# Routed experts: up weights split on chip into two float32r parts, three passes in place of one float32 product

## The chip, the cores and the metric

The kernel runs on one core of one Trainium2 chip. The metric is the device time of one execution in microseconds, taken as the median of several runs. All the times of instructions below come from one profiled execution.

## The reference, cut to what matters

The program is one inference step of a two-layer decoder trunk for 576 tokens (512 of a prompt and 64 of a sample group), width 1024. Layer 0 has a dense feed-forward part, layer 1 one of eight experts, of which each token uses two. Only this last part is touched:

```
def swiglu(x, w1, w3, w2):
    return (jax.nn.silu(x @ w1) * (x @ w3)) @ w2

    def moe(x, e_layer):
        ...
        logits = (xf @ moe_router[e_layer]).astype(f32)
        top_v, top_i = lax.top_k(logits, TOP_K)
        gw = jax.nn.softmax(top_v, axis=-1)
        comb = jnp.sum(jax.nn.one_hot(top_i, N_EXPERTS, dtype=f32) * gw[..., None], axis=1)
        y = jnp.zeros_like(xf)
        for e in range(N_EXPERTS):
            y = y + comb[:, e:e + 1].astype(x.dtype) * swiglu(xf, moe_w1[e_layer, e], moe_w3[e_layer, e], moe_w2[e_layer, e])
```

An expert has w1 and w3 of 1024 x 1408 (the "up" weights) and w2 of 1408 x 1024 ("down").

## The kernel before, in words

The tokens are sorted by expert into 16 blocks of 128 slots (`NBK`), written to `d_xs` by indirect DMAs, and each block is then run with the weights of its expert, which are read from HBM anew for each block. An expert's number is only known at run time, so SP loads it into a register ahead of each block.

A block's weights come in 18 units of up to 1 MiB (128 partitions x 2048 float32). Twelve are up units: groups g = 0, 1, 2 of 512, 512 and 384 hidden columns (`FG`), each with two halves q of the 1024 inputs and with w = 0, 1 for w1 and w3. The up units of group 2 are 1536 columns wide. Six are down units of two 128-row chunks f of w2 each, the last of one chunk. All of them go through one ring of 11 slots (`ring`), in the order in which PE uses them; SP issues unit n as soon as PE has finished unit n - 11 (`moe_used`).

In a block PE's order is written out in `moe_pe`: up 0, up 1, the transposes hT 0, up 2, hT 1, down 0, the transposes xT of the next block's tokens, hT 2, down 1, down 2. The tokens are the stationary operand (`XBT`) and the weights move. `moe_up_pe` (L2112) makes 4 matmuls per unit, 8 per PSUM bank. ACT takes Silu of the bank of w1 (`silu`, L2167), DVE multiplies it with the bank of w3 into `he_buf` (L2207), PE transposes that (hT, L2124), ACT copies it to `ht_buf` (`turned`, L2172), PE multiplies with the down weights (L2139). ACT copies the block's result (L2185) and sends it to `d_ys`. DVE prepares the next block's tokens from xT (L2197). Every engine runs its own instructions strictly in the order written; semaphores alone tie them together.

The dense layer 0 has long been computed with split operands: L470 multiplies float32r parts of the weights and of the tokens, 288 columns a time, in three passes (rounded x rounded, rounded x rest, rest x rounded). There ACT makes the rounded part (L455) and POOL or DVE the rest (L458, L533).

Of the kernel before, what the change touches and what calls it, by code (L numbers as in the profile page):

```python
# [14 lines left out]
P = 128  # L15
D = 1024
# [23 lines left out]
BLOCK_UNITS = UP_UNITS + DN_UNITS  # L40
RING = 11
# [144 lines left out]
def build(nc, A):  # L186

    with ExitStack() as ctx:
# [8 lines left out]
        SECOND = ("cmp_", "rope_", "at_", "sa_", "cw", "pages_", "qpages_", "qwin", "wo_", "w_out_", "ffn_norm", "moe_")  # L197
        shared, used = [], {True: 0, False: 0}

        def S(name):  # L200
            if name not in sems:
                part = name.startswith(FIRST)
                if part or name.startswith(SECOND):
# [50 lines left out]
        ring = put_at("ring", RING * 2048, mr)  # L254
        xn_tok = put_at("xn_tok", 5 * D, mx)
        xbt_buf = put_at("xbt_buf", 2 * D, mx)
        yb_buf = put_at("yb_buf", 2 * D, mx + 2 * D)
# [7 lines left out]
        wbc_buf = put_at("wbc_buf", 2 * D, mc + 13312)  # L265
        slot_buf = put_at("slot_buf", 16, mc + 15360, I32)
        ebt_buf = put_at("ebt_buf", NBK, mc + 15376, I32, 1)
        assert RING * 2048 <= 2560 + ARENA and 15392 <= NCH * T
# [1599 lines left out]
        XBT = xbt_buf[:, :].rearrange("p (m k t) -> p m k t", m=2, t=P)  # L1868
# [184 lines left out]
        def unit_of(b, u):  # L2053
            return (b * BLOCK_UNITS + u) % RING, (b * BLOCK_UNITS + u) // RING

        def up_unit(g, q, w):
            return 4 * g + 2 * q + w

        def moe_sp():
# [4 lines left out]
            for b in range(NBK):  # L2064
# [9 lines left out]
                for u in range(BLOCK_UNITS):  # L2074
                    slot, turn = unit_of(b, u)
                    if turn:
                        sp.wait_ge(S("moe_used"), b * BLOCK_UNITS + u - RING + 1)
                    if u < UP_UNITS:
                        g, q, w = u // 4, u // 2 % 2, u % 2
                        src = A["moe_up"][e * 8 + u] if g < 2 else A["moe_up2"][e * 4 + (u - 8)]  # L2080
                    else:
                        src = A["moe_dn"][e * DN_UNITS + (u - UP_UNITS)]
                    n = 2048 if u < 8 or u >= UP_UNITS else 4 * FG[2]
                    if u == BLOCK_UNITS - 1:
                        src, n = src[:, 0:D], D
                    sp.dma_start(ring[:, 2048 * slot:2048 * slot + n], src).then_inc(S(f"moe_unit_{slot}"), 16)
# [11 lines left out]
        def moe_up_pe(b, g):  # L2098
# [7 lines left out]
            for q in range(2):  # L2106
                for w in range(2):
                    u = up_unit(g, q, w)
                    slot, turn = unit_of(b, u)
# [17 lines left out]
        def moe_down_pe(b, g):  # L2127
# [4 lines left out]
            for f in range(4 * g, min(4 * g + 4, FC)):  # L2132
                u = UP_UNITS + f // 2
                slot, turn = unit_of(b, u)
                if f % 2 == 0:
                    pe.wait_ge(S(f"moe_unit_{slot}"), 16 * (turn + 1))
# [607 lines left out]
```

## Time and profile before

| | |
|---|---|
| median of 3 runs | 3269.13 us (3267.05 to 3274.06) |
| profiled execution | 3268.38 us, span 3266.6 us |
| PE busy in the span | 2788.6 us (85%) |
| DVE, ACT, POOL busy | 1121.7, 546.0, 356.0 us |
| float32 matmuls of the up weights (L2112) | 611.9 us busy, 1536 records |
| float32 matmuls of the down weights (L2139) | 307.4 us busy, 704 records |

Busy times are those of the engine over the whole span. A float32 matmul shows as two records with a weight load each, so 768 matmuls of the up weights are 1536 records. A float32r matmul shows as one record. In the chain of waits the first number of a row is its start in us from the span's start, the second how long it lasted.

### The profile page before, as it was taken

The page shows a single profiled execution, that of the slowest core. Times are in us where ns is not written, and L with a number is a line of the kernel's source. Part 1 is how long each engine was busy: PE and PEld are TensorE (multiplying, and loading weights), DVE is VectorE, ACT ScalarE, POOL GpSimd, SP SyncE. Part 2 cuts the span into 40 slices and gives each one's busy share as a digit, 9 for nine tenths or more (in the row PEclk, how much of TensorE's full clock was granted, in tenths as well). Part 3 has the DMA queues.
Part 4 walks back from the last instruction along what each step waited for, and adds up shares of the span by engine and source line. Part 5 has one row for each costly group of instructions (what it writes and reads, how often), then busy time and mean ns, then how long its engine had stood idle before and what let it go on. Part 6 is the DMA issues. An engine that isn't in the chain of part 4 may idle for free.

```text
span 3266.6 us, 36648 instructions
## 1 busy us (share of the span) xinstructions
PE 2788.6 (85%) x14880; PEld 2010.0 (62%) x14894; DVE 1121.7 (34%) x1676; ACT 546.0 (17%) x820; POOL 356.0 (11%) x160
## 2 busy tenths in 40 slices
PE   7977686897869999899648778885999999999994
PEld 6965583544769999799538654464454444544442
DVE  5314856367332032251376545843000000000002
ACT  3331100122222122222320011232000000000001
POOL 2320000000233333133000000011000000000001
PEclk9985786797889999899568878877999999999997
DMA  3210201210122343121012023013999988888883
GB/s 143 80 40 31 90 1 69 81 30 14 40 84 89 107 154 97 35 84 60 13 46 76 1 82 98 13 40 139 378 318 310 318 306 314 318 305 317 311 306 112
DMA packets 114970, 445.01 MB, mean 136 GB/s; under 512 B 12722, under 2 KB 47410, under 8 KB 86258
## 3 DMA queue, kind: packets, MB, share of 16 engines
q1 hardware_dynamic: 109874, 424.84, 38.0%
q0 software_dynamic: 2624, 9.44, 0.9%
q10 hardware_dynamic: 2304, 8.39, 0.6%
q8 instruction: 118, 1.93, 0.2%
q14 instruction: 50, 0.41, 0.0%
HBM read 410.28 MB, written 40.59 MB: 138 GB/s over the span
## 4 chain that ended last, share of the span: by engine, by line
PE 78%; DVE 15%; ACT 2%; issue 2%; DMA 1%; POOL 1%; DVEq 0%; SPq 0%; ACTq 0%; POOLq 0%; PEldq 0%
PE ps_buf L470 27%; PE ps_buf L2112 19%; PE ps_buf L2139 9%; PE ps_buf L1042 3%; PE ps_buf L1325 2%; PE ps_buf L1486 2%; PE ps_buf L1434 1%; PE ps_buf L1445 1%; PE ps_buf L1033 1%; DVE cols_buf L1140 1%; PE ps_buf L741 1%; PE ps_buf L1451 1%; PE ps_buf L1635 1%; DVE h_buf L529 1%; PE ps_buf L2124 1%
## 5 line engine op out<-in xcount | busy, mean ns | idle before, releaser
L470 PE MATMUL ps_buf<-xh_buf,whl_buf 128*128 128x288 f32 x3648 | 655.2, 301 | 71.1 <-POOLq L163 35.6
L2112 PE MATMUL ps_buf<-ring,xbt_buf 128*128 128x512 f32 (+1 forms) x1536 | 611.9, 558 | 3.4 <-DMA ring<-d_moe_up 3.4
L470 PEld LDWEIGHTS ps_buf<-xh_buf,whl_buf 128*128 128x128 f32 x3648 | 545.9, 191 | 79.8 <-issue 61.5
L2112 PEld LDWEIGHTS ps_buf<-ring,xbt_buf 128*128 128x128 f32 x1536 | 291.3, 191 | 313.0 <-issue 249.4
L470 PE MATMUL ps_buf<-xl_buf,whl_buf 128*128 128x288 f32 x1824 | 397.1, 299 | 0.0
L458 POOL TENSOR_TENSOR whl_buf<-arena,whl_buf 128x1024 fp32r<-128x1024 f32 (+1 forms) x114 | 289.0, 2535 | 582.6 <-ACTq L163 582.0
L2139 PE MATMUL ps_buf<-ring,ht_buf 128*128 128x512 f32 x704 | 307.4, 592 | 0.0
L470 PEld LDWEIGHTS ps_buf<-xl_buf,whl_buf 128*128 128x128 f32 x1824 | 297.8, 192 | 0.0
L2207 DVE TENSOR_TENSOR he_buf<-se_buf,ps_buf 128x512 f32<-128x512 f32 (+1 forms) x48 | 30.9, 644 | 769.1 <-ACT se_buf L2167 769.1
L2139 PEld LDWEIGHTS ps_buf<-ring,ht_buf 128*128 128x128 f32 x704 | 131.3, 190 | 153.1 <-issue 153.1
L455 ACT CAST whl_buf<-arena 128x1024 fp32r<-128x1024 f32 (+1 forms) x114 | 125.0, 1096 | 538.2 <-PE ps_buf L470 531.0
L458 POOL TENSOR_TENSOR whl_buf<-cols_buf,whl_buf 128x1024 fp32r<-128x1024 f32 x16 | 39.9, 2494 | 1264.9 <-ACTq L163 1264.5
L2167 ACT ACTIVATE se_buf<-ps_buf 128x512 f32<-128x512 f32 (+1 forms) x48 | 27.0, 562 | 595.5 <-PE ps_buf L2112 595.5
L470 PE MATMUL ps_buf<-hh_buf,whl_buf 128*128 128x288 f32 x704 | 122.9, 296 | 0.0
L2049 POOL DMA_INDIRECT yg_buf<-d_ys,slot_buf x10 | 9.4, 938 | 974.2 <-DMA d_ys<-yb_buf 958.4
L470 PEld LDWEIGHTS ps_buf<-hh_buf,whl_buf 128*128 128x128 f32 x704 | 103.4, 188 | 0.0
L2299 DVE TENSOR_TENSOR cols_buf<-arena,ps_buf 128x576 f32<-128x576 f32 x22 | 16.6, 755 | 211.4 <-PE ps_buf L470 211.4
L470 PE MATMUL ps_buf<-cols_buf,tab 128*128 128x288 f32 x144 | 50.6, 513 | 36.4 <-ACTq L163 15.7
L1486 PE MATMUL ps_buf<-arena,h_buf 128*128 128x512 f32 (+3 forms) x256 | 77.4, 447 | 2.5 <-ACTq L163 2.5
L1161 DVE TENSOR_TENSOR cols_buf<-cols_buf,ps_buf 128x512 f32<-128x512 f32 (+1 forms) x94 | 63.0, 670 | 43.5 <-PE ps_buf L1042 36.7
L470 PE MATMUL ps_buf<-hl_buf,whl_buf 128*128 128x288 f32 x352 | 75.7, 296 | 0.0
L1325 PE MATMUL ps_buf<-arena 128*128 128x296 f32 x256 | 69.9, 439 | 6.3 <-issue 6.3
(475 smaller groups left out, 3120.3 us busy)
## 6 DMA issues: line engine op xcount, KB each, us to landing
ring<-d_moe_up SPq DMA_DIRECT2D x128, 1024.0 KB, 7.2
ring<-d_moe_dn SPq DMA_DIRECT2D x80, 1024.0 KB, 7.0
ring<-d_moe_up SPq DMA_DIRECT2D x64, 768.0 KB, 6.5
arena<-d_w_in SPq DMA_DIRECT2D x54, 512.0 KB, 3.6
arena<-d_w SPq DMA_DIRECT2D x44, 512.0 KB, 3.7
arena<-d_w SPq DMA_DIRECT2D x16, 704.0 KB, 4.1
arena<-d_pages_c SPq DMA_DIRECT2D x64, 128.0 KB, 2.1
cols_buf<-d_w_out SPq DMA_DIRECT2D x16, 512.0 KB, 3.6
```

Source lines behind the costliest of these rows:

```text
L455: a(nc.scalar.copy(part(slot, 0, nk, size), src), *sig)
L458: g(nc.gpsimd.tensor_tensor(part(slot, 1, nk, size), src, part(slot, 0, nk, size).bitcast(F32), ALU.subtract), *sig)
L470: last = nc.tensor.matmul(ps_buf[0:rows, b + a_, 0:HALF], w, m[:, a_ * HALF:(a_ + 1) * HALF], start=start, stop=stop)
L529: v(ve.scalar_tensor_tensor(dst, x[:, k, :], w(k), rs, ALU.mult, ALU.mult), S(tag + ("_done" if final else "_scaled")))
L741: pe.matmul(o, onehot(h, n), R[0:4, RU, t0:t0 + n], start=True, stop=False)
L1033: last = pe.matmul(ps_buf[0:n, 4 * s_, q * n:q * n + n], M1[s_][0:n, q, 0:n], Dm[s_][0:n, q * n:q * n + n], start=True, stop=True)
L1042: last = pe.matmul(ps_buf[0:n, 4 * s_ + b, c], l_[s_][0:n, c], r_[s_][0:n, c], start=True, stop=True)
L1161: v(ve.tensor_tensor(D[s_][0:n, 0:4 * n], D[s_][0:n, 0:4 * n], ps_buf[0:n, 4 * s_ + b, 0:4 * n], ALU.add), *sig)
L1325: last = pe.matmul(bank(4 * j + 2 * g + half, 9 * 32 + 8), cw1[:, j, 8 * half + p_, :], ckb[:, :, j, g, 8 * p_:8 * p_ + 8], start=p_ == 0, ...
L1486: last = pe.matmul(ps_buf[:, out_banks(u) + g, P * c:SEQ], vaug[:, w, c, P * g:P * g + P], PTs[:, u % 2, g, CHUNK_AT[c]:CHUNK_AT[c] + n], ...
L2112: last = pe.matmul(ps_buf[:, o + w, 0:n], XBT[:, b % 2, 4 * q + k, :], ring[:, 2048 * slot + n * k:2048 * slot + n * k + n], start=q == 0 ...
L2139: last = pe.matmul(ps_buf[:, 6 + h, 0:512], HT[:, b % 2, f, :], ring[:, at:at + 512], start=f == 0, stop=f == FC - 1)
```

## The change

The up weights are no longer multiplied as float32. ACT copies each landed up unit to a float32r buffer (`high`, the rounded part), DVE subtracts this from the raw unit into a second one (`low`, the rest). PE multiplies in three passes with the rounded tokens `XBH` and their rest `XBL`. Down stays as it was. There are 4 raw up slots, 5 raw down slots and 3 pairs of split buffers in place of the ring of 11. A raw up slot is free when DVE has made its rest (`moe_lo`), a split pair when PE has used it (`moe_used`), a down slot when PE has used it (`moe_dn_used`). Tokens are split by DVE with two more operations per block. Some semaphores take over those of the dense layer, which are cleared by then.

```diff
@@ buffers
-ring = put_at("ring", RING * 2048, mr)                 # RING = 11
+up_buf = put_at("up_buf", RAW_UP * 2048, mr)           # RAW_UP, RAW_DN, SPLITS = 4, 5, 3
+dn_buf = put_at("dn_buf", RAW_DN * 2048, mr + RAW_UP * 2048)
+split_bufs = [...]                                     # three of 4096 columns, F32R
@@ moe_sp: the units of block b, in this order
-                for u in range(BLOCK_UNITS):
-                    slot, turn = unit_of(b, u)
-                    if turn:
-                        sp.wait_ge(S("moe_used"), b * BLOCK_UNITS + u - RING + 1)
...
+                for u in range(UP_UNITS):
+                    n = UP_UNITS * b + u
+                    if n >= RAW_UP:
+                        sp.wait_ge(S("moe_lo"), n - RAW_UP + 1)
+                    sp.dma_start(raw_up(n), A["moe_up"][e * 8 + u] if u < 8 else A["moe_up2"][e * 4 + (u - 8)])\
+                        .then_inc(S(f"moe_up_{n % RAW_UP}"), 16)
+                for u in range(DN_UNITS):
+                    m = DN_UNITS * b + u
+                    cols_n = D if u == DN_UNITS - 1 else 2 * D
+                    if m >= RAW_DN:
+                        sp.wait_ge(S("moe_dn_used"), m - RAW_DN + 1)
...
@@ moe_up_pe
-                    pe.wait_ge(S(f"moe_unit_{slot}"), 16 * (turn + 1))
+                    pe.wait_ge(S("moe_lo"), u + 1)
                     for k in range(4):
-                        last = pe.matmul(ps_buf[:, o + w, 0:n], XBT[:, b % 2, 4 * q + k, :],
...
+                        for x_, half in ((XBH, 0), (XBH, 1), (XBL, 0)):
+                            last = pe.matmul(ps_buf[:, o + w, 0:n], x_[:, b % 2, 4 * q + k, :], up_part(u, half)[:, c],
...
@@ moe_act
+            def high(n):
+                if n < UP_UNITS * NBK:
+                    ac.wait_ge(S(f"moe_up_{n % RAW_UP}"), 16 * (n // RAW_UP + 1))
+                    if n >= SPLITS:
+                        ac.wait_ge(S("moe_used"), n - SPLITS + 1)
+                    ac.copy(up_part(n, 0), raw_up(n)).then_inc(S("moe_hi"), 1)
+
+            for n in range(SPLITS):
+                high(n)
             for b in range(NBK):
+                n = UP_UNITS * b + SPLITS
+                for i in range(3):
+                    high(n + i)
                 silu(b, 0)
+                for i in range(3, 7):
+                    high(n + i)
                 silu(b, 1)
+                high(n + 7)
                 turned(b, 0)
+                for i in range(8, 11):
+                    high(n + i)
                 silu(b, 2)
+                high(n + 11)
                 turned(b, 1)
                 turned(b, 2)
@@ moe_dve
+                v(ve.tensor_tensor(XBT, src, nffn.unsqueeze(2).to_broadcast([P, KD, P]), ALU.mult))
+                v(ve.tensor_copy(XBH[:, b % 2], XBT))
+                v(ve.tensor_tensor(XBL[:, b % 2], XBT, XBH[:, b % 2].bitcast(F32), ALU.subtract), S("moe_xbt"))
+            def low(n):
+                if n < UP_UNITS * NBK:
+                    ve.wait_ge(S("moe_hi"), n + 1)
+                    ve.tensor_tensor(up_part(n, 1), raw_up(n), up_part(n, 0).bitcast(F32), ALU.subtract)\
+                        .then_inc(S("moe_lo"), 1)
...
+                for i in range(3, 7):
+                    low(n + i)
+                gated(b, 1)
+                for i in range(7, 11):
+                    low(n + i)
+                gated(b, 2)
+                low(n + 11)
                 if b + 1 < NBK:
                     xbt(b + 1)
```

Three places of the instruction order are shown. The first is ACT's, in one block from the second Silu to the copy of the result, before (`part_92` is `moe_used`, `part_61` is `moe_h`, `part_62` is `moe_hT`):

```order
L2167 ACTIVATE se_buf<-ps_buf 128x512 [waits part_61,part_92] x2
L2172 COPY ht_buf<-ps_buf 128x512 [waits part_62]
L2167 ACTIVATE se_buf<-ps_buf 128x384 [waits part_61,part_92]
L2172 COPY ht_buf<-ps_buf 128x512 [waits part_62]
L2172 COPY ht_buf<-ps_buf 128x384 [waits part_62]
L2185 COPY yb_buf<-ps_buf 128x1024 [waits part_92]
```

And the same place now (`part_76` to `part_79` are the landings `moe_up_0` to `moe_up_3`, `part_80` is `moe_used`, `part_47` is `moe_hT`, `part_46` is `moe_h`):

```order
L2187 ACTIVATE se_buf<-ps_buf 128x512 [waits part_46,part_80]
L2200 CAST split_buf_72<-up_buf 128x1536 [waits part_80,part_78]
L2192 COPY ht_buf<-ps_buf 128x512 [waits part_47]
L2200 CAST split_buf_73<-up_buf 128x1536 [waits part_80,part_79]
L2200 CAST split_buf_71<-up_buf 128x2048 [waits part_80,part_76]
L2200 CAST split_buf_72<-up_buf 128x2048 [waits part_80,part_77]
L2187 ACTIVATE se_buf<-ps_buf 128x384 [waits part_46,part_80]
L2200 CAST split_buf_73<-up_buf 128x2048 [waits part_80,part_78]
L2192 COPY ht_buf<-ps_buf 128x512 [waits part_47]
L2192 COPY ht_buf<-ps_buf 128x384 [waits part_47]
```

Between the copy of group 0 and the third Silu (128x384) there are now three casts; the two that are 2048 wide are up units 0 and 1 of the next block.

The second place is DVE's, around the third product of a block (`he_buf` 128x384), now (`ex_raw_free` is `moe_hi`, `ex_h` is `moe_silu`); before, only the three products and one `xbt_buf` operation stood in a block:

```order
L2250 TENSOR_TENSOR he_buf<-se_buf,ps_buf 128x512 [waits part_47,ex_h]
L2242 TENSOR_TENSOR split_buf_72<-up_buf,split_buf_72 128x1536 [waits ex_raw_free]
L2242 TENSOR_TENSOR split_buf_73<-up_buf,split_buf_73 128x1536 [waits ex_raw_free]
L2242 TENSOR_TENSOR split_buf_71<-up_buf,split_buf_71 128x2048 [waits ex_raw_free]
L2242 TENSOR_TENSOR split_buf_72<-up_buf,split_buf_72 128x2048 [waits ex_raw_free]
L2250 TENSOR_TENSOR he_buf<-se_buf,ps_buf 128x384 [waits part_47,ex_h]
L2242 TENSOR_TENSOR split_buf_73<-up_buf,split_buf_73 128x2048 [waits ex_raw_free]
L2235 TENSOR_TENSOR xbt_buf<-ps_buf,small 128x1024 [waits ex_raw_in_1]
L2236 CAST xbh_buf<-xbt_buf 128x1024 [waits dve_chain]
L2237 TENSOR_TENSOR xbl_buf<-xbt_buf,xbh_buf 128x1024 [waits dve_chain]
```

Here too the rests of units 0 and 1 of the next block stand ahead of this block's third product.

The third place is SP's, from a block's last down unit to the next block's first up unit, now (`part_82` is `moe_dn_used`, `ex_out_free` is `moe_lo`):

```order
L2105 ISA [waits part_82]
L2105 DMA dn_buf<-d_moe_dn 128x1024
L2084 TENSOR_LOAD ebt_buf
L2084 ISA x2
L2091 DMA xb_buf<-d_xs 128x1024 [waits ex_raw_in_1]
L2097 ISA [waits ex_out_free]
L2097 DMA up_buf<-d_moe_up 128x2048
```

The order of the transfers is that of before; what the last down unit waits for is new: with five down slots it is the block's own first down unit, where it was the use of the eleventh unit back.

## Rows read from the trace of the kernel before

**Rows 1.** The chain of waits, from the experts' start: start us, length us, engine, line

```profile
2271.45 7.50 DMA ring<-d_moe_up
2279.08 29.68 PE ps_buf L2112 x64
2309.20 10.32 PE ps_buf L2112 x32
...
2340.05 27.47 PE ps_buf L2112 x64
2367.95 10.32 PE ps_buf L2112 x32
...
2398.80 27.47 PE ps_buf L2112 x64
```

**Rows 2.** Groups by line and form: xcount | busy us, mean ns of one

```profile
L2112 PE MATMUL ps_buf<-ring,xbt_buf 128*128 128x512 f32 x1024 | 444.1, 594 | 3.4 <-DMA ring<-d_moe_up 3.4
L2207 DVE TENSOR_TENSOR he_buf<-se_buf,ps_buf 128x384 f32<-128x384 f32 x16 | 8.9, 554 | 159.4 <-ACT se_buf L2167 159.4
```

**Rows 3.** Timeline of PE, layer 1's output projection: eight times x4 and x2 between

```profile
2180.88 0.70 PE L470 MATMUL ps_buf<-xh_buf,whl_buf 128*128 128x288 f32 x4
2181.41 0.43 PE L470 MATMUL ps_buf<-xl_buf,whl_buf 128*128 128x288 f32 x2
...
2187.28 0.43 PE L470 MATMUL ps_buf<-xh_buf,whl_buf 128*128 128x288 f32 x2
```

**Rows 4.** Groups by line and form: wide operations of ACT and DVE in SBUF

```profile
L455 ACT CAST whl_buf<-arena 128x1024 fp32r<-128x1024 f32 x98 | 102.9, 1050 | 436.5 <-PE ps_buf L470 429.3 <-DMA arena<-d_w 6.8
L455 ACT CAST whl_buf<-arena 128x1408 fp32r<-128x1408 f32 x16 | 22.0, 1377 | 101.7 <-PE ps_buf L470 101.7
...
L533 DVE TENSOR_TENSOR xl_buf<-h_buf,xh_buf 128x576 fp32r<-128x576 f32 x24 | 18.2, 758 | 3.5
L1850 DVE CAST xh_buf<-split_buf 128x576 fp32r<-128x576 f32 x16 | 11.4, 714 | 0.6
L1231 DVE TENSOR_TENSOR arena<-arena,small 128x1024 f32<-128x1024 f32 x4 | 4.9, 1224 | 0.1
L1254 DVE TENSOR_TENSOR h_buf<-h_buf,small 128x1280 f32<-128x1280 f32 x4 | 6.0, 1492 | 0.1
L2301 DVE TENSOR_TENSOR hl_buf<-cols_buf,hh_buf 128x576 fp32r<-128x576 f32 x22 | 55.0, 2499 | 0.8
```

**Rows 5.** Timeline of a block's down part, steady state

```profile
2613.55 7.03 PE L2139 MATMUL ps_buf<-ring,ht_buf 128*128 128x512 f32 x16
2620.42 1.04 PE L2095 MATMUL ps_buf<-tab,xb_buf 128*128 128x128 f32 x8
2621.30 0.49 PE L2124 MATMUL ps_buf<-tab,he_buf 128*128 128x128 f32 x3
2621.62 12.18 PE L2139 MATMUL ps_buf<-ring,ht_buf 128*128 128x512 f32 x28
```

**Rows 6.** Timeline of the experts' first transfers and first work

```profile
2270.45 0.33 SPq L2068 DMA_DIRECT2D xb_buf<-d_xs  x1
2270.82 0.43 SPq L2072 DMA_DIRECT2D xb_buf<-d_xs  x1
2271.45 13.80 SPq L2086 DMA_DIRECT2D ring<-d_moe_up  x12
2273.73 1.97 PE L2095 MATMUL ps_buf<-tab,xb_buf 128*128 128x128 f32 x8 [23.21 <-DMA xb_buf<-d_xs]
2279.08 6.51 PE L2112 MATMUL ps_buf<-ring,xbt_buf 128*128 128x512 f32 x10 [3.38 <-DMA ring<-d_moe_up]
```

**Rows 7.** Stretches: busy us of PE, PEld, DVE, ACT, POOL; granted clock, DMA share, GB/s

```profile
2271.00:2280.00 9.00, 2.89 (x9) 2.07 (x10) 1.23 (x1) 0.00 (x0) 0.00 (x0) 0.50 0.92 362
2280.00:2290.00 10.00, 10.00 (x21) 4.39 (x20) 0.00 (x0) 0.00 (x0) 0.00 (x0) 0.85 1.01 426
2290.00:2300.00 10.00, 10.00 (x24) 4.37 (x23) 0.69 (x1) 0.60 (x1) 0.00 (x0) 1.00 1.01 416
...
2457.00:2516.00 59.00, 59.00 (x161) 28.68 (x160) 3.16 (x4) 4.19 (x7) 0.00 (x0) 1.00 0.91 312
```

More of the change, by code:

```diff
@@ L39 @@
 DN_UNITS = 6
-BLOCK_UNITS = UP_UNITS + DN_UNITS
-RING = 11
+RAW_UP, RAW_DN, SPLITS = 4, 5, 3
 NEG = -1e30
@@ L202, in S @@
                 part = name.startswith(FIRST)
+                if name.startswith("moe_") and FFN_ONLY:
+                    sems[name] = S(FFN_ONLY.pop())
+                    return sems[name]
                 if part or name.startswith(SECOND):
@@ L2051, in moe_gather_pool, with up_cols, raw_up, up_part @@
                         .then_inc(S(f"moe_yg_{i % 2}"), 16)
-        def unit_of(b, u):
-            return (b * BLOCK_UNITS + u) % RING, (b * BLOCK_UNITS + u) // RING
+        def up_cols(n):
+            return 2048 if n % UP_UNITS < 8 else 4 * FG[2]
+        def raw_up(n):
+            return up_buf[:, 2048 * (n % RAW_UP):2048 * (n % RAW_UP) + up_cols(n)]
+        def up_part(n, which):
+            return split_bufs[n % SPLITS][:, 2048 * which:2048 * which + up_cols(n)]
         def up_unit(g, q, w):
@@ L2107, in moe_up_pe @@
                 for w in range(2):
-                    u = up_unit(g, q, w)
-                    slot, turn = unit_of(b, u)
-                    pe.wait_ge(S(f"moe_unit_{slot}"), 16 * (turn + 1))
+                    u = UP_UNITS * b + up_unit(g, q, w)
+                    pe.wait_ge(S("moe_lo"), u + 1)
                     for k in range(4):
-                        last = pe.matmul(ps_buf[:, o + w, 0:n], XBT[:, b % 2, 4 * q + k, :],
-                                         ring[:, 2048 * slot + n * k:2048 * slot + n * k + n],
-                                         start=q == 0 and k == 0, stop=q == 1 and k == 3)
+                        c = slice(n * k, n * k + n)
+                        for x_, half in ((XBH, 0), (XBH, 1), (XBL, 0)):
+                            last = pe.matmul(ps_buf[:, o + w, 0:n], x_[:, b % 2, 4 * q + k, :], up_part(u, half)[:, c],
+                                             start=q == 0 and k == 0 and x_ is XBH and half == 0,
+                                             stop=q == 1 and k == 3 and x_ is XBL)
                     last.then_inc(S("moe_used"), 1)
@@ L2132, in moe_down_pe @@
             for f in range(4 * g, min(4 * g + 4, FC)):
-                u = UP_UNITS + f // 2
-                slot, turn = unit_of(b, u)
+                m = DN_UNITS * b + f // 2
                 if f % 2 == 0:
-                    pe.wait_ge(S(f"moe_unit_{slot}"), 16 * (turn + 1))
+                    pe.wait_ge(S(f"moe_dn_{m % RAW_DN}"), 16 * (m // RAW_DN + 1))
                 for h in range(2):
-                    at = 2048 * slot + D * (f % 2) + 512 * h
-                    last = pe.matmul(ps_buf[:, 6 + h, 0:512], HT[:, b % 2, f, :], ring[:, at:at + 512],
+                    at = 2048 * (m % RAW_DN) + D * (f % 2) + 512 * h
+                    last = pe.matmul(ps_buf[:, 6 + h, 0:512], HT[:, b % 2, f, :], dn_buf[:, at:at + 512],
                                      start=f == 0, stop=f == FC - 1)
                 if f % 2 or f == FC - 1:
-                    last.then_inc(S("moe_used"), 1)
+                    last.then_inc(S("moe_dn_used"), 1)
         def moe_pe():
```

62 lines of the change are left out of this document (35 added, 27 removed).

## The prediction

> **What bounds the kernel now.** I read the chain of waits first, then the groups by line, then a timeline of one block, then the stretches. The chain [rows 1] shows that the experts' part is one unbroken row of PE work: up 0 and 1 (27.47 us), up 2 (10.32), down, and again, with a period of 2398.80 - 2340.05 = 58.75 us for each of 16 blocks. The only wait for a transfer is the first, 3.4 us in all [rows 2]. The stretches say the same: PE is busy throughout at the full clock of 2.4 GHz, the DMA engines move 312 GB/s (the last stretch) [rows 7], and ACT and DVE are nearly idle. Right at the start the same engines moved 416 to 426 GB/s, so the steady 312 is what PE asks for and not what they can do. 312 GB/s over 58.75 us are 18.3 MB a block; at 420 GB/s they would take 43.7 us. So PE's passes bound this part, and anything that makes PE wait is added to the time.
>
> **What the change removes: PE passes.** A block has 64 + 32 records for up, together 27.47 + 10.32 = 37.79 us [rows 1]; that is 0.429 us a record of 512 columns, two records a matmul. Now each of the 32 + 16 matmuls is three float32r passes: 96 of 512 columns and 48 of 384. No row shows a float32r pass of 512. The nearest is 288: between 2180.88 and 2187.28 stand 48 of them, 6.40 / 48 = 133.3 ns each [rows 3], where 288 columns at 2.4 GHz are 120. The excess of 13.3 ns may be fixed (226.7 and 173.3 ns), may grow with the columns (237 and 178 ns), or may be the weight load's and vanish behind a longer pass (213.3 and 160 ns). I take it as fixed, the middle: 96 x 0.2267 + 48 x 0.1733 = 30.1 us, 7.7 us less a block, 123 us in 16 blocks. The ends are 31.3 us (6.5 less, 104 in all) and 28.2 us (9.6 less, 154 in all).
>
> The Trainium skill, "TensorE: Matmul & The Clock Gate", section "Back-to-back issue gap", gives N/2.4 + 2.5 ns for a matmul at full clock. That would be 122.5 ns at 288, and the trace has 133.3, so it does not agree for these passes; with it the up part would be 28.5 us and the total 25 us below mine.
>
> **What it adds on ACT and DVE, in the steady flow.** ACT casts took 1050 ns for 1024 columns and 1377 for 1408, so 0.852 ns a column: 1.92 us for 2048 and 1.49 for 1536. DVE took 1224 ns for 1024 and 1492 for 1280: 1.047 ns a column, 2.30 us and 1.76 us. That its float32r results cost no more is seen at 576 columns, 758 ns. All of this is [rows 4]. A split pair goes round cast, rest, PE and four hand-overs of some 0.1 us: 1.92 + 2.30 + 12 x 0.2267 + 0.3 = 7.2 us, with three pairs 2.4 us a unit, against PE's 2.72. So within a block the splits stay just ahead of PE. Per block ACT gets 8 x 1.92 + 4 x 1.49 = 21 us and DVE 25 us and some 2 us for the tokens, in a period of over 50. Cost there: none. Its bounds: zero, or, if DVE ran as in its slowest row (2499 ns for 576 [rows 4], in a part of the kernel where POOL works beside it; POOL is idle here [rows 7]), far more; that is a rival below.
>
> **What it adds by its order: one stall a block.** This is the term that decides. Three facts from the order of instructions and the code meet:
>
> 1. SP's transfers are in order, and the last down unit of block b (the sixth, with five slots) waits until PE has used the first down unit of the same block. All of block b+1's transfers stand behind it. Call this moment t0.
> 2. ACT's third Silu of block b stands behind the casts of up units 0 and 1 of block b+1.
> 3. DVE's third product of block b stands behind the rests of the same two units. PE's hT 2 needs that product, and down 1 and down 2 follow it.
>
> So PE's second half of down waits for weights of the next block that cannot be asked for before t0. The length: from t0 the queue is down 5 (0.5 MiB), tokens (0.5), up 0 (1), up 1 (1). The start of the experts has the same sequence of 0.5, 0.5 and 1 MiB: first issue at 2270.45, PE starts on up 0 at 2279.08, of which about 0.1 is the hand-over, so 8.5 us [rows 6]. The single tokens' transfer took 2273.73 - 2270.45 = 3.3 us, of which 0.52 MB at 420 GB/s are 1.25, so 2.0 are fixed; by this up 0 lands after 2.0 + 2.1 MB at 420 GB/s (5.0) = 7.0. Up 1 is 2.5 us behind. With 0.1 for the semaphore it lands between 9.6 and 11.1 us; I take 10.4. Then the cast 1.9, the rest 2.3, the product 0.55 [rows 2] and 0.3 of hand-overs: PE can begin hT 2 at t0 + 15.4. What covers it: after t0 PE has half of down 0 left, 3.43 us, and xT, 0.9; in the trace 2613.55 + 3.43 = 2616.98 is t0 and hT 2 began at 2621.30 [rows 5], 4.3 us. The stall is 15.4 - 4.3 = 11.1 us; 10.3 to 11.8 by the two ways for the landing, and I allow 9 to 13.
>
> Behind the stalled hT 2 stand 28 records of down, the copy of the result on ACT and, behind that, the casts from unit 3 of the next block on. These are not late on top: units 0 to 2 are split and raw 3 to 6 landed by the time PE comes to them, 12 us later.
>
> The stall also costs clock. At the experts' start PE was idle, the granted clock was 0.50 of full (1.2 GHz) in the first stretch and 0.85 in the next [rows 7], and the first 64 records took 29.68 us against 27.47 later [rows 1]: 2.2 us lost. After 11 us of idleness I expect the same fall each time, on down 1. Bounds: zero, if the gap leaves the clock up, and 3.4 us. I take 2.1.
>
> The last block has nothing to split for a next one, so 15 stalls: 15 x (11.1 + 2.1) = 198 us.
>
> **The first block** starts later by one cast and one rest, 1.92 + 2.30 + 0.1 = 4.3 us, on the chain. The token split (three operations of 1.2 to 1.3 us) is done while up 0 travels.
>
> **DMA.** A block's 18.3 MB over the new period of 58.75 - 7.7 + 13.2 = 64.3 us are 285 GB/s, below the 416 to 426 shown. Down units 0 to 4 are asked for during up 2 and land about when down 0 starts to use them, the last around t0.
>
> The Trainium skill, "HBM Reference", section "Specifications (TRN2)", gives some 358 GB/s as a core's share. The first full stretches show 416 to 426, so with one core streaming the trace does not show that limit. If it held, the 3.1 MB ahead of up 1's landing would take 1.3 us longer and the total would be 20 us above mine.
>
> **The sum**, against the profiled execution (3268.4 us, 0.7 below the median of the runs, 1.8 outside its span): 3268.4 - 123 + 198 + 4 = 3347.4. I predict 3347 us.
>
> **The rivals.**
> - A, the stall is not there or is hidden, and the passes decide: 3268.4 - 123 + 4 = 3149 us. For it: everything that ACT, DVE and DMA do fits into a block by its sums, and a unit's split stays ahead of PE. Against it: the queue of SP in the shown order has no way to ask for unit 0 before t0. The break-even is (123 - 4) / 15 = 7.9 us a block; the stall would have to be shorter than that, clock included. Chance 0.05.
> - B, cheap passes and a cheap stall: passes at 213 and 160 ns (-154), a stall of 10.3 us with no loss of clock (+155): 3268.4 - 154 + 155 + 4 = 3273 us, near no change. With somewhat less stall it is just faster. For it: the excess of 13.3 ns may vanish; against it: the clock fell whenever PE idled at the start. Chance 0.06.
> - C, DVE becomes the bound. If DVE took its slowest row's 4.3 ns a column, 22,528 columns a block are 98 us: over 39 us more than now for each block, at least 3890 us. Against it: the POOL row of the stretches is zero. Chance 0.01.
> - D, half of it: passes at 213 and 160 ns but the stall and its clock as forecast: 3268.4 - 154 + 198 + 4 = 3316 us. This lies in the range, as does its counterpart with 104 us (3366).
> - E, the change does nothing to PE, as when float32r passes were made like float32 ones. Against it: 133 ns for 288 columns [rows 3], where the float32 records of 512 take 429. Below 0.01.
>
> **How the numbers follow.** The forecast with its own bounds (D among them) has 0.88, A 0.05, B 0.06, C and E 0.01. Passes and stall move the time by -30 and +20, and by -30 to +30 us, the clock by -31 and +20. Not all of them fall on one side, and I reach from 3300 to 3385. A measurement of this kernel can tell about 0.2% (6.5 us) from no change. Faster by more: A and half of B, 0.08. Within: 0.03. Slower: 0.89.
>
> **What would show it.** Right: the chain of waits has in each block but the last a break ahead of hT 2, released by DVE's product, with ACT's third Silu and DVE's third product waiting for a cast and a rest of the next block, and those casts for the transfer. A block's period is near 64 us, up 0 and 1 take near 21.8 us and up 2 near 8.3, the clock falls in each gap, and DMA moves near 285 GB/s. Wrong: a period under 58 us, a DMA queue that is busy ahead of t0 with the next block's units, PE gaps within the up part (then the splits are slower than priced), or a pass of 512 columns far from 0.23 us.

## The result, and the profile after

The changed kernel takes 3372.73 us (median of 4 runs, 3364.47 to 3380.85), the kernel before 3270.84 us in the same comparison. The ratio is 1.0312, interval 1.0296 to 1.0328: 3.1% slower. The forecast was 3347 us. The profiled execution was the slowest of the four, 3380.85 us with a span of 3379.0.

The page of the changed kernel: busy us of the engines, and the granted clock in 40 slices. DVE has 432 us more, ACT 332, and the clock now has dips in the experts' part (the last 13 slices), where the kernel before has a 9 in every slice but the last:

```profile
PE 2714.2 (80%) x15662; PEld 2155.2 (64%) x15662; DVE 1553.9 (46%) x1900; ACT 878.3 (26%) x1012; POOL 355.4 (11%) x160
PEclk9975886895899999997689679688998998899897
```

The chain of waits in the experts' part, start and length in us; it answers to [rows 1]:

```profile
2277.72 7.33 DMA up_buf<-d_moe_up
2287.00 2.30 DVE split_buf L2242
2289.44 24.02 PE ps_buf L2133 x96
...
2424.77 22.16 PE ps_buf L2133 x96
2447.36 8.39 PE ps_buf L2133 x48
2456.20 3.45 PE ps_buf L2159 x8
2462.14 9.46 DMA up_buf<-d_moe_up
2477.27 13.48 PE ps_buf L2159 x28
2490.75 22.16 PE ps_buf L2133 x96
```

Before, the chain ran through PE alone. Now it leaves PE in every block but the last, right after the first down unit (x8), goes through a transfer of up weights and comes back at hT 2 and the 28 records of down 1 and 2. A block takes 65.98 us here; from 2380.09 to 3305.13, the starts of up 2 in blocks 1 and 15, it is 66.07 on average, against 58.75.

The same moment two blocks later on the engines, starts and lengths in us (in brackets, how long the engine had been idle and who ended that). The first down unit, from the chain, begins at 2589.47 and takes 3.45, so t0, the moment when PE has used it, is 2592.92:

```profile
2589.47 3.45 PE ps_buf L2159 x8
```

```profile
2602.60 1.90 ACT L2200 CAST split_buf<-up_buf 128x2048 fp32r<-128x2048 f32 x1 [18.26 <-DMA up_buf<-d_moe_up]
2605.09 1.90 ACT L2200 CAST split_buf<-up_buf 128x2048 fp32r<-128x2048 f32 x1 [0.59 <-DMA up_buf<-d_moe_up]
2606.89 0.48 ACT L2187 ACTIVATE se_buf<-ps_buf 128x384 f32<-128x384 f32 x1
```

```profile
2604.53 2.29 DVE L2242 TENSOR_TENSOR split_buf<-up_buf,split_buf 128x2048 fp32r<-128x2048 f32 x1 [18.40 <-ACT split_buf L2200]
2607.02 2.29 DVE L2242 TENSOR_TENSOR split_buf<-up_buf,split_buf 128x2048 fp32r<-128x2048 f32 x1 [0.20 <-ACT split_buf L2200]
2609.23 0.55 DVE L2250 TENSOR_TENSOR he_buf<-se_buf,ps_buf 128x384 f32<-128x384 f32 x1
```

```profile
2609.83 0.90 PE L2145 MATMUL ps_buf<-tab,he_buf 128*128 128x128 f32 x3 [12.62 <-DVE he_buf L2250]
2610.53 13.51 PE L2159 MATMUL ps_buf<-dn_buf,ht_buf 128*128 128x512 f32 x28
```

The granted clock right after that gap (the last three numbers of a stretch are the clock, the DMA share and GB/s) is the lower level, 1.2 GHz:

```profile
2609.80:2612.00 2.20, 2.17 (x5) 1.37 (x6) 2.20 (x2) 0.64 (x2) 0.00 (x0) 0.50 1.05 376
```

Read from the bottom: PE sat idle for 12.62 us until DVE's third product. The product was not waiting for the Silu, done 2 us earlier, but stood behind two rests, and these behind two casts of the next block's weights, ahead of which ACT had waited 18 us for their transfer. ACT and DVE both sat idle while the operation that PE needed stood in their queues, behind one that could not run.

Where the time went, in the experts' part of the two profiled executions:

| term | forecast | measured |
|---|---|---|
| float32r passes in place of float32 | -123 | 16 x (37.79 - 22.16 - 8.37) = -116 |
| PE idle ahead of hT 2, 15 blocks | +167 | +183.6 |
| clock after the gap, 28 records | +32 | 218.8 - 192.3 = +26.5 |
| hT 2 after the gap, until down 1 starts (one block's, times 15) | in the line above | 15 x (0.70 - 0.32) = +6 |
| first block's split | +4 | 11.72 - 7.63 = +4 |
| sum | +79 | +104 |

By the chains, from the first weight transfer to PE's last down record the part took 949.0 us before and 1055.4 after, 106.4 more. The other 6 us between the two spans arose ahead of it: the first transfer starts at 2271.45 before and 2277.72 after, though nothing that runs before it is changed; in the profiled executions of the other kernels below it started anywhere between 2266.2 and 2285.2, so I put it down to the spread of executions.

### The profile page after: what moved, and what is told of

Read it like the earlier page. It is cut to its first block, busy times and chain, and to the rows that moved or that the text cites. A ratio compares the mean times of both kernels' runs of the same rounds, so it can differ in the third digit from the quotient of the medians.

```text
span 3379.0 us, 38816 instructions
## 1 busy us (share of the span) xinstructions
PE 2714.2 (80%) x15662; PEld 2155.2 (64%) x15662; DVE 1553.9 (46%) x1900; ACT 878.3 (26%) x1012; POOL 355.4 (11%) x160
## 4 chain that ended last, share of the span: by engine, by line
PE 72%; DVE 15%; DMA 6%; ACT 3%; issue 3%; SPq 1%; POOL 1%; DVEq 0%; ACTq 0%; POOLq 0%; PEldq 0%
PE ps_buf L481 27%; PE ps_buf L2133 15%; PE ps_buf L2159 8%; DMA up_buf<-d_moe_up 4%; PE ps_buf L1053 3%; PE ps_buf L1336 2%; PE ps_buf L1497 2%; PE ps_buf L1456 1%; PE ps_buf L1445 1%; PE ps_buf L1044 1%; ACT split_buf L2200 1%; PE ps_buf L2145 1%; PE ps_buf L1462 1%; DVE cols_buf L1151 1%; PE ps_buf L1646 1%
## 5 line engine op out<-in xcount | busy, mean ns | idle before, releaser
L2242 DVE TENSOR_TENSOR split_buf<-up_buf,split_buf 128x2048 fp32r<-128x2048 f32 (+1 forms) x192 | 405.8, 2114 | 545.7 <-ACT split_buf L2200 544.4
L2133 PE MATMUL ps_buf<-split_buf,xbh_buf 128*128 128x512 f32 (+1 forms) x1536 | 458.9, 380 | 7.5 <-DVE split_buf L2242 7.5
L2200 ACT CAST split_buf<-up_buf 128x2048 fp32r<-128x2048 f32 (+1 forms) x192 | 338.3, 1762 | 406.1 <-DMA up_buf<-d_moe_up 308.5
L2159 PE MATMUL ps_buf<-dn_buf,ht_buf 128*128 128x512 f32 x704 | 334.6, 634 | 0.0
L2133 PEld LDWEIGHTS ps_buf<-split_buf,xbh_buf 128*128 128x128 f32 x1536 | 284.6, 188 | 58.4 <-issue 15.0
L2133 PE MATMUL ps_buf<-split_buf,xbl_buf 128*128 128x512 f32 (+1 forms) x768 | 288.0, 375 | 0.0
L2159 PEld LDWEIGHTS ps_buf<-dn_buf,ht_buf 128*128 128x128 f32 x704 | 143.1, 208 | 169.9 <-issue 169.9
L2145 PE MATMUL ps_buf<-tab,he_buf 128*128 128x128 f32 x176 | 33.2, 315 | 183.6 <-DVE he_buf L2250 183.6
L2133 PEld LDWEIGHTS ps_buf<-split_buf,xbl_buf 128*128 128x128 f32 x768 | 144.5, 188 | 22.4
L2145 PEld LDWEIGHTS ps_buf<-tab,he_buf 128*128 128x128 f32 x176 | 23.9, 159 | 190.3 <-DVE he_buf L2250 187.2
## 6 DMA issues: line engine op xcount, KB each, us to landing
dn_buf<-d_moe_dn SPq DMA_DIRECT2D x80, 1024.0 KB, 11.1
```

The costliest lines, as they stand in the source:

```text
L2133: last = pe.matmul(ps_buf[:, o + w, 0:n], x_[:, b % 2, 4 * q + k, :], up_part(u, half)[:, c], start=q == 0 and k == 0 and x_ is XBH and ha ...
L2145: last = pe.transpose(ps_buf[:, 4 + gi % 2, P * c:P * c + P], HE[:, gi % 2, P * c:P * c + P], ident)
L2159: last = pe.matmul(ps_buf[:, 6 + h, 0:512], HT[:, b % 2, f, :], dn_buf[:, at:at + 512], start=f == 0, stop=f == FC - 1)
L2200: ac.copy(up_part(n, 0), raw_up(n)).then_inc(S("moe_hi"), 1)
L2242: ve.tensor_tensor(up_part(n, 1), raw_up(n), up_part(n, 0).bitcast(F32), ALU.subtract)\
```

## The experiments

Ratios are to the kernel before on the same chip. "The changed kernel" is the one above, 1.0312.

### The new order undone: third Silu, third product, copies and tokens ahead of the next block's splits

```diff
@@ moe_act
-                for i in range(8, 11):
-                    high(n + i)
+                high(n + 8)
                 silu(b, 2)
-                high(n + 11)
                 turned(b, 1)
                 turned(b, 2)
+                for i in range(9, 12):
+                    high(n + i)
@@ moe_dve
-                for i in range(7, 11):
+                for i in range(7, 9):
                     low(n + i)
                 gated(b, 2)
-                low(n + 11)
                 if b + 1 < NBK:
                     xbt(b + 1)
+                for i in range(9, 12):
+                    low(n + i)
```

> Only the order on ACT and DVE is changed: the third Silu, the third product, the copies of hT 1 and hT 2 and the next block's tokens stand ahead of the casts and rests of the next block's units 0, 1 and 2. The slots and SP's waits stay as in the changed kernel. Theory (PE waits for the third product only because the next block's splits stand ahead of it): the gap of some 12 us ahead of hT 2 is gone in all blocks, the clock stays at full, a block takes 58.75 - 7.3 = 51.5 us, and the whole near 3270 + 4 - 16 x 7.3 = 3157 us (ratio to the kernel before 0.965). Rival (SP's late request is the cause whatever stands behind it, so the wait only moves from hT 2 to up unit 0 or 1 of the next block): up 0 lands some 9.5 us after the first down unit is used, its cast and rest end at 14, PE would come to it at 17 or later; if the wait moves anyway, the time stays above 3270 us. Rival 2 (float32r passes at full load are slower or the splits can't keep ahead): gaps within the up part, 3200 us or more.

Measured 3157.05 us, ratio 0.9664 (0.9647 to 0.9680). The chain, starts and lengths, and a stretch of this kernel (busy us of PE, PEld, DVE, ACT, POOL, granted clock, DMA share, GB/s):

```profile
2646.78 22.17 PE ps_buf L2133 x96
2669.39 8.37 PE ps_buf L2133 x48
2678.19 6.87 PE ps_buf L2159 x16
2686.26 12.02 PE ps_buf L2159 x28
2698.28 22.16 PE ps_buf L2133 x96
```

```profile
2400.00:2500.00 100.00, 100.00 (x403) 70.93 (x402) 58.14 (x36) 48.39 (x37) 0.00 (x0) 1.00 0.95 362
```

A block takes 51.50 us, PE is busy throughout at full clock, and the 28 records take 12.02 us. The order alone was worth 6.5% of the time of the kernel before (1.0312 less 0.9664), and this kernel is 3.4% faster than that one. All the work of the change is still in it, and SP still asks for the next block's units as late as in the changed kernel. So the split work costs nothing that shows beyond the first block, where the first cast and rest are still on the chain.

### Six down slots in place of five

```diff
-RAW_UP, RAW_DN, SPLITS = 4, 5, 3
+RAW_UP, RAW_DN, SPLITS = 4, 6, 3
-dn_buf = put_at("dn_buf", RAW_DN * 2048, mr + RAW_UP * 2048)
+dn_buf = put_at("dn_buf", RAW_DN * 2048 - 1024, mr + RAW_UP * 2048)
```

> Only the down slots are changed, from five to six (the sixth half as wide, since only the last down unit comes to it), so that the last down unit waits for the block before and SP can ask for the next block's up units during up 2 or earlier. The orders of ACT and DVE stay as in the changed kernel, so the third Silu still stands behind the casts of the next block's units 0 and 1. Theory (both are needed, the late request and what stands behind it): the next units have landed when ACT comes to their casts, which then only wait for split pairs that PE has left at the end of up 2; cast, rest, rest and product of some 7.5 us after the end of up 2 are less than down 0 and the transposes that cover them (8.2 us), so at most 1 us of gap is left: 3157 to 3175 us. Rival (the order alone makes the stall): the gap of 12 us stays and the time is near 3370 us.

Measured 3336.49 us, ratio 1.0220 (1.0203 to 1.0237). A miss: I had asked when SP may go on, and not what it would then have in front. SP's DMAs, the first cast of the next block, and two stretches of this kernel:

```profile
2618.25 3.48 SPq L2105 DMA_DIRECT2D dn_buf<-d_moe_dn  x6
2622.88 48.17 SPq L2097 DMA_DIRECT2D up_buf<-d_moe_up  x8
```

```profile
2641.21 1.90 ACT L2200 CAST split_buf<-up_buf 128x2048 fp32r<-128x2048 f32 x1 [15.54 <-DMA up_buf<-d_moe_up]
```

```profile
2600.00:2610.00 10.00, 10.00 (x45) 8.12 (x44) 4.85 (x3) 6.17 (x4) 0.00 (x0) 1.00 0.33 122
2620.00:2630.00 10.00, 10.00 (x58) 9.70 (x57) 5.96 (x4) 4.32 (x5) 0.00 (x0) 1.00 1.02 419
```

All six down units leave within 3.5 us and unit 0 of the next block is asked for 4.6 us after the first of them, but it stands behind those 5.5 MiB, and its cast starts 18.3 us after its issue. They leave so late because only four raw up slots exist, each held until DVE has made the rest: in the stretch from 2600, during up 0, the DMA engines are a third busy, and in the one from 2620, during up 2, they are full. The gap ahead of hT 2 went from 183.6 to 146.0 us in sum. So SP's wait with five slots was one cause of the late landing, and the bunched transfers are a second behind it.

### Four down slots

```diff
-RAW_UP, RAW_DN, SPLITS = 4, 5, 3
+RAW_UP, RAW_DN, SPLITS = 4, 4, 3
```

> Only the down slots are changed, from five to four. Now the last down unit waits until PE has used the second down unit of its block, 3.43 us later than with five. Theory (the gap is measured from the moment SP is let go): the gap ahead of hT 2 grows from 12.2 to between 14.5 and 15.7 us (the fifth unit is under way meanwhile, and one more transfer of 1 MiB stands in the queue), 15 times: 35 to 60 us more than the changed kernel's 3373, so 3408 to 3433 us. Rival (the gap is the length of cast and rest alone, or DVE's own load): no change, 3373 us.

Measured 3421.95 us, ratio 1.0472 (1.0455 to 1.0490), as expected. PE's waits in this kernel and, second, in the changed one: us in total, times, longest:

```profile
PE ps_buf L2145 <- DVE he_buf L2250: 229.8, 15, 15.8
```

```profile
PE ps_buf L2145 <- DVE he_buf L2250: 183.6, 15, 13.3
```

3.1 us more a block for a release that comes 3.43 us later: with four and five slots the gap moves with that release.

### Two passes in place of three

```diff
-                        for x_, half in ((XBH, 0), (XBH, 1), (XBL, 0)):
+                        for x_, half in ((XBH, 0), (XBH, 1)):
```

> The third pass (rounded weights by the rest of the tokens) is left out, so the up products are less exact; all else is as in the changed kernel. Theory (PE's up part and the gap add up, since the gap is counted from the first down unit): each block loses 32 passes at 231 ns... and 16 at 174 ns, 7.39 + 2.79 = 10.2 us, if the splits keep up. They don't quite: with PE at 1.85 us a unit the three pairs go round in 1.92 + 2.30 + 1.85 + 0.3 = 6.4 us, 2.12 us a unit, and DVE alone needs 2.3 us a unit; so the up part becomes DVE's and costs about 8 x 2.4 + 4 x 1.85 = 26.6 us less what the three units split ahead save (some 1.5), 25 against 30.5: 5 to 6 us a block, 80 to 95 us in all: 3278 to 3293 us. Rival (PE's passes still set the up part): 16 x 10.2 = 163 us less, 3210 us. Rival 2 (the gap takes up what the passes leave, since the transfers set the period): near 3373 us.

Measured 3316.49 us, ratio 1.0148 (1.0131 to 1.0164). Both rivals are excluded, but the size was off: some 56 us came off the changed kernel's time in place of 80 to 95. The chain of this kernel, from one first down unit to the next:

```profile
2940.61 3.45 PE ps_buf L2159 x8
2946.22 9.77 DMA up_buf<-d_moe_up
2961.66 13.37 PE ps_buf L2159 x28
...
2978.92 3.72 DVE split_buf L2242 x2
...
2988.59 6.26 DMA up_buf<-d_moe_up
2998.19 4.62 PE ps_buf L2133 x16
3003.25 3.45 PE ps_buf L2159 x8
```

This block takes 62.64 us; over 14 blocks it is 62.1 on average, 4.0 less than in the changed kernel and not 5 to 6. The gap ahead of hT 2 is as before (185.4 us in sum). What is new are waits within the up part: PE waits there for DVE's rests 63.9 us in sum, and behind those rests the chain goes, through the four raw slots, to a second transfer. With a third of the passes gone PE is no longer what bounds it, so the margin that the splits had over PE in the changed kernel was a small one.

### Only ACT's order, and only DVE's

First the third Silu alone moved ahead of the next block's casts (the copies stay):

```diff
-                for i in range(8, 11):
-                    high(n + i)
+                high(n + 8)
                 silu(b, 2)
-                high(n + 11)
+                for i in range(9, 12):
+                    high(n + i)
```

> Only ACT's order is changed: the third Silu of a block stands ahead of the casts of the next block's units 0 and 1. DVE's third product still stands behind the rests of those two. Theory (either of the two orders holds PE alone): the rest of unit 1 ends as late as before, so the gap stays at 12.2 us and the time at 3373 us, within 10. Rival (ACT's Silu is what PE waits for in the end): the gap and the time fall, towards 3157 us.

Measured 3373.16 us, ratio 1.0313 (1.0288 to 1.0338), and a gap ahead of hT 2 of 180.4 us in sum: nothing, as expected. Then the third product alone moved ahead of the next block's rests:

```diff
-                for i in range(7, 11):
+                for i in range(7, 9):
                     low(n + i)
                 gated(b, 2)
-                low(n + 11)
+                for i in range(9, 12):
+                    low(n + i)
```

> Only DVE's order is changed: the third product of a block stands ahead of the rests of the next block's units 0 and 1. ACT's third Silu still stands behind the casts of those two. Theory (either order holds PE alone): the product no longer waits for the rest of unit 1 (2.3 us) but starts when the Silu is done (0.5 us after the cast), so the gap is 1.8 us shorter, 15 times: 27 us less than 3373, 3346 us, within 10. Rival (DVE's order alone is the cause): the gap goes and the time is near 3157 us.

Measured 3370.28 us, ratio 1.0304 (1.0277 to 1.0332), not told apart from the changed kernel and outside what I expected. PE in this kernel:

```profile
2666.52 0.90 PE L2145 MATMUL ps_buf<-tab,he_buf 128*128 128x128 f32 x3 [9.60 <-DVE he_buf L2250]
2668.51 14.19 PE L2159 MATMUL ps_buf<-dn_buf,ht_buf 128*128 128x512 f32 x28 [1.09 <-ACT ht_buf L2192]
```

The gap ahead of hT 2 did shrink (151.9 us in sum, 2.1 less a block), but then the copy of hT 1 was late, since it stands behind the cast of unit 2 on ACT (16.4 us in sum), and the 28 records took 227.6 us in sum against 218.8. Of some 32 us about 6 are left. So neither edit alone frees PE. No kernel here has just these two edits: the first experiment, which frees it, moves the copies and the tokens ahead of the splits as well, and the late copy of hT 1 says that the copies belong to what had to move.

### PE kept at work in the gap

```diff
                     moe_xT_pe(b + 1)
+                    for _ in range(12):
+                        nc.tensor.matmul(ps_buf[:, 4 + (3 * b + 2) % 2, 0:512], ident,
+                                         ht_buf[:, E1 * (b % 2):E1 * (b % 2) + 512], start=True, stop=True)
                 moe_hT_pe(b, 2)
```

> The changed kernel with 12 float32 matmuls of 512 columns more on PE, ahead of hT 2 in each block but the last; their result is overwritten. At full clock they last 12 x 0.858 = 10.3 us and lie in the gap of 12.2. Theory (after the gap PE runs at half clock for a while, which costs 1.75 us in the 28 records of down and 0.4 in the transposes before them): the clock stays up, the 28 records take 12.03 us in place of 13.8, and the time falls by 15 x 2.1 = 32 us to 3341 us. Rival (the slow first records after the gap are due to something else, such as the transfers of that moment): the 28 records stay at 13.8 us and the time at 3373 us.

Measured 3350.55 us, ratio 1.0244 (1.0219 to 1.0269). More work on PE made the kernel 22 us faster. The 28 records take 199.4 us in sum in place of 218.8: 12.0 to 12.3 in 12 blocks, 13.7 in the other four. In one of those four, PE and the granted clock:

```profile
2660.83 0.55 PE L2145 MATMUL ps_buf<-tab,he_buf 128*128 128x128 f32 x3 [2.48 <-DVE he_buf L2253]
```

```profile
2655.00:2658.00 3.00, 3.00 (x8) 1.14 (x6) 2.29 (x1) 2.42 (x3) 0.00 (x0) 1.00 1.00 423
2662.00:2664.00 2.00, 2.00 (x3) 0.69 (x3) 2.00 (x2) 0.00 (x0) 0.00 (x0) 0.50 0.98 389
```

The fill ends 2.5 us before hT 2 can start, and after that idle the clock still fell to 0.50; from 2666 on it was 1.00 again. The four blocks with slow records are the four in which PE had idled longest ahead of hT 2 (2.30, 2.48, 2.66 and 3.05 us; 1.22 to 2.11 in the other eleven with a gap). So the slow records are the clock's doing, and some 7 us of what I had expected went to these four blocks. The 22 us are somewhat less than the 26.5 + 6 counted above.

### The slots alone, without the splits

This is the kernel before with four up slots and five down slots, each freed when PE has used it:

```diff
-            return (b * BLOCK_UNITS + u) % RING, (b * BLOCK_UNITS + u) // RING
+            if u < UP_UNITS:
+                n = b * UP_UNITS + u
+                return n % RAW_UP, n // RAW_UP
+            m = b * DN_UNITS + u - UP_UNITS
+            return RAW_UP + m % RAW_DN, m // RAW_DN
```

> The kernel before with float32 products and no splits, but with the slots of the changed kernel: four for up and five for down, each unit freed by PE's use, in place of the ring of eleven. So SP lets the next block's units go as late as in the changed kernel (after the first down unit), but nothing of this block stands behind them. Theory (the late request hurts only through what stands behind it): up 0 lands some 9 us after the first down unit is used, PE comes to it at 16.7 us; no gap, 3270 us, within 7. Rival (the slot plan costs by itself): up to 15 x 2 to 12 us more, 3300 to 3450 us.

Measured 3266.78 us, ratio 0.9995 (0.9983 to 1.0006). No cost, though the request is as late as in the changed kernel. Down 0 and SP's first transfer for the next block:

```profile
2616.74 7.03 PE L2151 MATMUL ps_buf<-ring,ht_buf 128*128 128x512 f32 x16
2621.46 0.34 SPq L2084 DMA_DIRECT2D xb_buf<-d_xs  x1
```

The tokens leave 1.3 us after the first half of down 0, and up 0 follows at 2621.99. The late request is harmless here, where nothing of the running block stands behind it.

### New order and six slots together

The edits of the first two experiments in one kernel.

> The order of the first experiment (third Silu, third product and the tokens ahead of the next block's casts and rests) together with six down slots. Theory (with the new order nothing on PE waits, so an earlier request has nothing left to hide): the same as the new order alone, 3157 us, within 4. Rival (with SP let go earlier the next block's units are split earlier and the time falls again): 3150 us or less. Rival 2 (the transfers bunch as with six slots alone, where 5.5 MiB of down units stood ahead of the next block's unit 0): PE waits for unit 0, 1 or 2 of a block, 3165 us or more.

Measured 3152.16 us, ratio 0.9663 (0.9650 to 0.9676), the same as with the new order alone (0.9664). From the second block on PE waits for nothing in either.

### Two up units of the next block ahead of this block's down units

```diff
@@ moe_sp
+                ups(b, e, range(2 if b else 0, UP_UNITS))
+                if b + 1 < NBK:
+                    e_next = sp.value_load(ebt_buf[0:1, b + 1:b + 2], min_val=0, max_val=7)
+                    ups(b + 1, e_next, range(2))
                 for u in range(DN_UNITS):
```

> The changed kernel with its orders of ACT and DVE and its slots, but SP issues the first two up units of the next block ahead of this block's down units, in place of behind them. It undoes the late landing alone. Theory (the gap is counted from the landing of the next block's units 0 and 1, whatever lets SP go): they land in up 2, casts and rests only wait for split pairs, product 3 is ready before down 0 ends, and the gap ahead of hT 2 is gone. The first down unit lands 2 MiB later (5 us), some 1 to 3 us after PE comes to it. A block takes 51.5 + 1 to 3 us, the whole 3170 to 3205 us. Rival (the order on ACT and DVE is enough to keep the gap, also with the units there): 3330 us or more.

Measured 3353.27 us, ratio 1.0286 (1.0261 to 1.0311): the rival's range, but not for the rival's reason. PE and ACT in this kernel (the window ends within the last group of PE, which has 28 records in 14.35 us):

```profile
2641.30 7.11 PE L2166 MATMUL ps_buf<-dn_buf,ht_buf 128*128 128x512 f32 x16 [1.67 <-DMA dn_buf<-d_moe_dn]
2658.89 13.49 PE L2166 MATMUL ps_buf<-dn_buf,ht_buf 128*128 128x512 f32 x26 [9.29 <-ACT ht_buf L2199]
```

```profile
2656.45 1.90 ACT L2207 CAST split_buf<-up_buf 128x2048 fp32r<-128x2048 f32 x1 [15.44 <-DMA up_buf<-d_moe_up]
2658.26 0.96 ACT L2199 COPY ht_buf<-ps_buf 128x512 f32<-128x512 f32 x2
```

The gap ahead of hT 2 is gone, as expected. In its place down 1 waits 9.3 us (136.7 in sum) for the copy of hT 1, which stands on ACT behind the cast of unit 2, and unit 2 was the first not to be asked for early. I had counted units 0 and 1 because product 3 stands behind those, and had not looked one instruction further on ACT. Two kernels test that reading.

### Three units ahead; two units ahead and the copy moved

The first asks for three units early (`range(3)`). The second keeps two and puts `turned(b, 1)` ahead of `high(n + 11)` on ACT.

> As the experiment before, but SP issues three up units of the next block (0, 1 and 2) ahead of this block's down units. With two, the third product was in time, but the copy of hT 1 stood on ACT behind the cast of unit 2, which landed last of all: 9.3 us of gap. Theory (PE always waits for whatever stands behind the last late landing): with three units ahead nothing that PE needs stands behind a late one; what is left is the first down unit, which lands behind 3 MiB, some 3 to 4 us after PE comes to it: a block takes 51.5 + 3 to 4 us, the whole 3157 + 15 x 3 to 4 = 3202 to 3217 us, within 15. Rival (the gap has another cause on ACT and stays): 3330 us or more.

Measured 3249.86 us, ratio 0.9927 (0.9906 to 0.9949). The chain, and the granted clock at the start of the 16 records:

```profile
2678.19 9.24 DMA dn_buf<-d_moe_dn
2687.57 9.46 PE ps_buf L2166 x16
2698.23 12.02 PE ps_buf L2166 x28
```

```profile
2687.50:2690.00 2.50, 2.43 (x3) 1.18 (x4) 1.69 (x1) 0.00 (x0) 0.00 (x0) 0.50 1.00 423
```

The waits on ACT and DVE are gone. What is left is the first down unit, 66.4 us in sum, 4.4 a block, near what was expected. The time is some 33 us above the upper figure because I had left out the clock: the 16 records after this wait take 9.46 us here and not 6.87, and over the blocks they take 32 us more in sum.

> As the experiment with two units ahead, but the copy of hT 1 stands ahead of the cast of unit 2 on ACT; the copy of hT 2 still stands behind it. Theory (the wait moves to the next instruction that stands behind unit 2's landing): PE does hT 2 and down 1 (6.9 us) and then waits for the copy of hT 2; of the gap of 9.3 us some 3 are left, with the 1.7 for the first down unit 4.7 us a block: 3157 + 15 x 4.7 = 3228 us, within 15. Rival (the copy of hT 1 was the last thing late): 3157 + 15 x 1.7 = 3183 us or less. Rival 2 (its order doesn't matter): 3353 us.

Measured 3227.39 us, ratio 0.9868 (0.9837 to 0.9899), the time that I expected. PE's waits in this kernel from 2300 to 3270 us, in total, times, longest:

```profile
PE ps_buf L2166 <- ACT ht_buf L2199: 37.2, 15, 3.6
PE ps_buf L2166 <- DMA dn_buf<-d_moe_dn: 14.7, 14, 1.8
```

The wait moved on to the copy of hT 2, which excludes both rivals. That the time came out to the microsecond is luck: the waits are 51.9 us in sum, 3.5 a block and not 4.7, and the clock, which I had left out again, makes up for it (the records of down take 325.7 us here and 307.4 with the new order). Each instruction that PE needs, taken out from behind a late one, brings the time down: 3353 and 3227 here, and 3157 in the first experiment, where the units are asked for late again but none of PE's needs stands behind them.

## Why the prediction was right

The direction and the mechanism were right, the time was 26 us short, inside the range. By its own steps:

- **PE passes.** 22.16 us for 96 passes are 230.8 ns at 512 columns, 8.37 for 48 are 174.4 ns at 384; I had 226.7 and 173.3. With 133.3 at 288 the excess over the columns at 2.4 GHz is 13.3, 14.4 and 17.5 ns: neither fixed nor in proportion, between my middle and my dear end. This term gave 116 us in place of 123. By N/2.4 + 2.5 ns, which the Trainium skill, "TensorE: Matmul & The Clock Gate", section "Back-to-back issue gap", gives for the gap of an isolated matmul, a pass would take 216 and 162.5 ns; the passes here take 15 and 12 ns more, so the trace does not agree.
- **Casts and rests.** 1.90 and 2.29 us, 1.48 and 1.76, as priced (1.92 and 2.30, 1.49 and 1.76). In the steady flow they cost nothing: PE does not wait within the up part after the first block's start, and the new order alone gives 51.5 us a block. The margin is small, as the kernel with two passes shows.
- **The stall.** Its three facts are borne out: the release (later release, longer gap; slots alone, no cost), and the two orders on ACT and DVE (neither alone frees PE; both together with the copies and the tokens do). I had missed that the copies of hT 1 and hT 2 stand behind a cast too, that of unit 2. The size was the term that was most off: 12.2 us and not 11.1. The step was the landing. I had taken up 1 to land 10.4 us after t0; in the block shown its cast started 12.2 us after it. Up 1 was 2.5 us behind up 0 as reckoned, so the loss lies ahead of up 0, whose cast started 9.7 us after t0. SP issued up 0 only 1.6 us after t0 (2594.56): it sends the last down unit, loads the expert's number and sends the tokens first, and I had counted only their bytes. The DMA engines had finished the earlier down units by then and moved nothing from 2593 to 2594, and then they were slow to come back to the 426 GB/s that they moved from 2600 on:

```profile
2593.00:2594.00 1.00, 1.00 (x3) 0.38 (x2) 0.00 (x0) 0.00 (x0) 0.00 (x0) 1.00 0.00 0
2595.00:2596.00 1.00, 1.00 (x4) 0.41 (x3) 0.00 (x0) 0.00 (x0) 0.00 (x0) 1.00 1.07 246
```

  Why they moved 246 GB/s while fully busy is not shown.
- **The clock.** 1.8 us on the 28 records and 0.4 ahead of them, against 2.1. That it is the clock is shown by the granted clock of 0.50 after the gap and by filling the gap.
- **DMA.** The changed kernel moves 274 to 279 GB/s in its blocks (285 forecast). With the new order it is 348 to 362 GB/s, with the DMA engines busy for 92 to 95% of the time, and PE still does not wait for them.
- **Rival A** (passes decide, 3149 us) is the kernel with the new order: 3157 us. I had granted its sums and held against it that SP cannot ask for unit 0 before t0. The sums were right; but the late request is still there in the kernel with the new order and costs nothing, so what separates the two kernels is what stands behind it on ACT and DVE.

The points that I missed lie in the experiments: behind a removed wait stood a second one, in the transfers (six slots) and on ACT (two units ahead).

## What to carry to other kernels

When work for the next block is written into an engine's queue, look at what of this block stands behind it, and at when its input can land at all: the casts and rests of three units in the wrong place cost 6.5% of the time of the kernel before here, though with the right order ACT and DVE are busy for less than 60% of the time. Ask this for each instruction behind, since removing one wait shows the next. A transfer's landing time was set by what stood ahead of it in the queue as much as by when it was let go: 18.3 us from issue to cast behind six down units.

## What the runs showed of the hardware that I had not expected

- A float32r pass costs more than its columns at full clock, by 13.3 ns at 288 columns, 14.4 at 384 and 17.5 at 512, while the two float32 records of a product with 512 columns take 0.858 us together, almost exactly four times its columns at full clock (0.853 us). Three passes are 19% faster than the float32 product at 512 columns, not 25%.
- With the fill, idle times of 2.30 to 3.05 us on PE were followed by the lower clock and slow records (four blocks), and idle times of 1.22 to 2.11 us were not (eleven blocks), though PE had been busy at full clock until then. The 28 records after a long gap took between 13.02 and 14.67 us in the changed kernel.
- Useless matmuls in the gap made the kernel faster (1.0244 against 1.0312).

Not tried: splitting the down weights too, and a plan with more raw up slots.
